# The first two dense halves take the input times the norm's weights, and the norm's factor is applied at their eviction

## The reference, cut to what matters

```python
def rms_norm(x, g):
    y = x * lax.rsqrt(jnp.mean(x * x, axis=-1, keepdims=True) + EPS)
    return y * g

h = rms_norm(x, norm_g[0])
proj = h @ w_in          # its first 1024 columns are lru_x, the next 1024 lru_g, then the rest
xc = causal_conv(lru_x, conv_w) + conv_b      # per channel, 4 taps
...                      # gates, scan, two other mixers, ffn, two more layers
```

## Time and profile before

| | us |
|---|---|
| median of 3 runs | 2349.78 (2349.71 to 2351.39) |
| the profiled execution | 2353.49 |
| its span in the trace | 2351.7 |
| PE busy | 2281.4 (97%) |
| DVE busy | 1474.1 (63%) |
| ACT busy | 919.0 (39%) |

### The profile page before, as it was taken

How to read it: one execution, slowest core, us unless ns; L and a number is a source line. 1 busy time by engine, 2 the same in 40 slices (tenths; PEclk the granted TensorE clock), 3 DMA queues, 4 the chain that set the end, 5 groups by cost and what they waited for, 6 DMA issues and landing times.

```text
span 2351.7 us, 33475 instructions
## 1 busy us (share of the span) xinstructions
PE 2281.4 (97%) x14276; PEld 1983.6 (84%) x14276; DVE 1474.1 (63%) x1936; ACT 919.0 (39%) x1331; POOL 248.5 (11%) x238
## 2 busy tenths in 40 slices
PE   8899998999999999999999999999999999998999
PEld 7899885789998888888859888888888888978998
DVE  6585548577768776756877776335754433976554
ACT  6653435454454222124454212223322222545443
POOL 0030000201111101010020101000100101201110
PEclk9999998899999999999999999999999999999999
DMA  6544370356654454433202544223454322622543
GB/s 239 188 178 163 128 261 33 125 198 233 238 192 167 161 210 187 171 126 113 108 1 108 215 170 188 108 76 114 187 197 162 143 99 84 177 72 93 195 180 108
DMA packets 35393, 358.24 MB, mean 152 GB/s; under 512 B 4029, under 2 KB 6269, under 8 KB 9004
## 3 DMA queue, kind: packets, MB, share of 16 engines
q1 hardware_dynamic: 31788, 343.54, 38.9%
q0 software_dynamic: 3456, 12.56, 1.9%
HBM read 353.11 MB, written 1.13 MB: 151 GB/s over the span
## 4 chain that ended last, share of the span: by engine, by line
PE 88%; DVE 7%; ACT 3%; issue 1%; DMA 1%; POOLq 0%; SPq 0%; DVEq 0%; ACTq 0%
PE psum L861 25%; PE psum L860 25%; PE psum L862 25%; PE psum L924 2%; PE psum L923 2%; PE psum L925 2%; PE psum L1200 1%; PE psum L1226 1%; DVE ring_r L1938 1%; PE psum L1271 1%; DVE rr L1948 1%; DVE small L2465 1%; DVE zT L1967 1%; PE psum L1155 1%; DVE zT_r L1978 0%
## 5 line engine op out<-in xcount | busy, mean ns | idle before, releaser
L860 PE MATMUL psum<-arena_r 128*128 128x256 f32 (+1 forms) x3144 | 1058.8, 337 | 10.4 <-DVE ring_r L1938 4.3
L862 PE MATMUL psum<-arena_r,ring_r 128*128 128x256 f32 (+1 forms) x3144 | 1052.7, 335 | 0.0
L861 PE MATMUL psum<-zT_r,arena_r 128*128 128x256 f32 (+1 forms) x2592 | 848.4, 327 | 0.0
L1440 ACT ACTIVATE arena_r<-ring 128x2048 fp32r<-128x2048 f32 (+1 forms) x252 | 473.3, 1880 | 700.3 <-PE psum L862 651.2
L1938 DVE TENSOR_TENSOR ring_r<-ring,arena_r 128x2048 fp32r<-128x2048 f32 (+1 forms) x252 | 569.5, 2261 | 215.4 <-ACT arena_r L1440 214.5
L860 PEld LDWEIGHTS psum<-arena_r 128*128 128x128 f32 x3144 | 592.2, 188 | 85.7 <-issue 13.1
L862 PEld LDWEIGHTS psum<-arena_r,ring_r 128*128 128x128 f32 x3144 | 595.1, 189 | 65.3
L861 PEld LDWEIGHTS psum<-zT_r,arena_r 128*128 128x128 f32 x2592 | 489.6, 189 | 43.9
L861 PE MATMUL psum<-arena_r 128*128 128x256 f32 (+1 forms) x1128 | 373.4, 331 | 0.0
L2091 DVE CUSTOM_DVE_ANT_0 psum<-arena,cb 128x1024 f32<-128x1024 f32 x256 | 318.0, 1301 | 0.0
L861 PEld LDWEIGHTS psum<-arena_r 128*128 128x128 f32 x1128 | 212.4, 188 | 22.1
(11 more groups left out here) (316 smaller groups left out, 2234.3 us busy)
## 6 DMA issues: line engine op xcount, KB each, us to landing
ring<-in_wf SPq DMA_DIRECT2D x75, 2048.0 KB, 7.6
ring<-in_w SPq DMA_DIRECT2D x41, 2048.0 KB, 7.7
arena<-in_w SPq DMA_DIRECT2D x72, 1024.0 KB, 9.5
ring<-in_wf SPq DMA_DIRECT2D x10, 1536.0 KB, 6.5
ring<-in_w SPq DMA_DIRECT2D x5, 1024.0 KB, 5.3
arena<-strip_scratch POOLq DMA_DIRECT2D x1, 2048.0 KB, 9.5
arena<-rpb_scratch POOLq DMA_DIRECT2D x16, 128.0 KB, 11.3
xT<-in_x SPq DMA_DIRECT2D x1, 1024.0 KB, 5.7
```

The lines of the kernel that those rows point to most:

```text
L860: mm(b[c][:, at], whc, xh[:, k, at], start=(k == ks[0]), stop=False)
L861: mm(b[c][:, at], whc, xl[:, k, at], start=False, stop=False)
L862: last = mm(b[c][:, at], wlc, xh[:, k, at], start=False, stop=(k == ks[-1]))
L1440: A(W_hi[h % NHI][:, 0:n], ring[:, half_slot(h)], ACT.Identity).then_inc(sig("w_hi"), 1)
```

## The change

The norm's tile `norm0` and its eight matmuls go. Instead:

- The DMA queue of SP has the first half of chunk 0 right behind the one-hot table, then the 8 columns of weights of the first norm by themselves (`first_gain_in`), then `x`, the constants, the rest of `vec`, and the second half of chunk 0 as before.
- ACT begins with `w_hi(0)`, makes 8 high parts of `x * g` (`F_hi`), the 8 squares, `w_hi(1)`, loads the table of the root, takes the root (`first_root`), makes `w_hi(2)`, and only then the 8 `z_high`.
- DVE makes `w_lo(0)`, 8 low parts of `x * g` (`F_lo`), adds the squares up itself (7 adds), makes `w_lo(1)`, the reciprocal, evicts the two tiles of `lru_x0` times the factor (`first_x(0)`), makes `w_lo(2)`, goes through the ten rounds of `norm_z` and `z_low`, and evicts `lru_x1` in the same way.
- PE does halves 0 and 1 on `F_hi` and `F_lo`, with one product of ones and the summed squares before the seventh tile of features; halves 2 to 7 and all others on the normed input as before.

```diff
     add("strip", None, "V")
-    add("norm0", None, "A")
-    split_pairs("lru_x", 2, W8_LRU_X, "AA")
+    split_pairs("lru_x", 1, W8_LRU_X, "VV")
+    split("lru_x2", "lru_x3", w8(W8_LRU_X + 1), "AA")
...
+        F_hi, F_lo = part(18456, KT, S), part(20504, KT, S)
+        first_total = psum[:, 7 * BANK:7 * BANK + S]
...
-        PE_SUM = (0, 2, 4)
-        SUMS = (5, 6, 7, 8, 9), (4, 5, 6, 7, 8)
+        PE_SUM = (2, 4)
+        SUMS = (0, 5, 6, 7, 8, 9), (4, 5, 6, 7, 8)
...
-            sp.dma_start(cst[:, 0:CST_FIRST], d["cst"][:, 0:CST_FIRST]).then_inc(sig("cst_in"), 16)
-            sp.dma_start(xT[:, :, 0:S], d["x"].rearrange("k p t -> p k t")).then_inc(sig("x_in"), 16)
             arr, idx, _ = CHUNKS[0][0]
             sp.dma_start(ring[:, 0:HALF], d[arr][idx, :, 0:HALF]).then_inc(sig("first_half_in"), 16)
-            sp.dma_start(vec[:, :], d["vec"]).then_inc(sig("vec_in"), 16)
+            sp.dma_start(V("norm_g", 0, KT), d["vec"][:, 0:KT]).then_inc(sig("first_gain_in"), 16)
+            sp.dma_start(xT[:, :, 0:S], d["x"].rearrange("k p t -> p k t")).then_inc(sig("x_in"), 16)
+            sp.dma_start(cst[:, 0:CST_FIRST], d["cst"][:, 0:CST_FIRST]).then_inc(sig("cst_in"), 16)
+            sp.dma_start(vec[:, KT:VN], d["vec"][:, KT:VN]).then_inc(sig("vec_in"), 16)
...
-            norm(0)
+            def first_ready(k):
+                pe.wait_ge(sig("first_lo"), k + 1)
+                if k == 6:
+                    pe.wait_ge(sig("cst_in"), 16)
+                    pe.wait_ge(sig("norm_sum_x"), 1)
+                    mm(first_total, C("ones"), rr[:, 0:S], start=True, stop=True).then_inc(sig("first_total"), 1)
+
+            split_features(HALF_AT["lru_x0"], S, F_hi, F_lo, before=first_ready, both=True)
+            split_features(HALF_AT["lru_x1"], S, F_hi, F_lo)
             pe.wait_ge(sig("vec_in"), 16)
-            for c in range(4):
...
+            for c in range(2, 4):
+                split_features(HALF_AT[f"lru_x{c}"], S, h_hi, z_lo, before=split_ready(0, 0) if c == 2 else None,
+                               both=c == 2)
...
+            w_hi(0)
+            act.wait_ge(sig("first_gain_in"), 16)
+            act.wait_ge(sig("x_in"), 16)
+            for k in range(KT):
+                A(F_hi[:, k, :], xT[:, k, 0:S], ACT.Identity, scale=V("norm_g", k, 1)).then_inc(sig("first_hi"), 1)
+            for k in range(KT):
+                square(0, k, HALF_TOK[0], xT, "norm_sq")
+            w_hi(1)
             act.wait_ge(sig("cst_in"), 16)
             sqrt_table()
-            norm(0, xT, lambda k: act.wait_ge(sig("x_in"), 16), before=lambda: w_hi(0))
-            w_hi(1)
+            act.wait_ge(sig("first_total"), 1)
+            A(rt[:, 0:S], first_total, ACT.Sqrt, scale=1.0 / D, bias=C("eps")).then_inc(sig("first_root"), 1)
+            w_hi(2)
+            z_high(0, 0)
             act.wait_ge(sig("vec_in"), 16)
...
             def lru_x(c):
-                copy_tiles(f"lru_x{c}", 2, lambda j: A_xp[:, 2 * c + j, 3:S + 3])
+                if c >= 2:
+                    copy_tiles(f"lru_x{c}", 2, lambda j: A_xp[:, 2 * c + j, 3:S + 3])
...
+            w_lo(0)
+            dve.wait_ge(sig("first_gain_in"), 16)
             dve.wait_ge(sig("x_in"), 16)
-            w_lo(0)
-            norm(0, xT, lambda k: V("norm_g", k, 1))
+            for k in range(KT):
+                dve.wait_ge(sig("first_hi"), k + 1)
+                v.scalar_tensor_tensor(out=F_lo[:, k, :], in0=xT[:, k, 0:S], scalar=V("norm_g", k, 1),
+                                       in1=F_hi[:, k, :].bitcast(f32), op0=ALU.mult, op1=ALU.subtract)\
+                    .then_inc(sig("first_lo"), 1)
+            for k in range(1, KT):
+                add_square(0, k, HALF_TOK[0])
             w_lo(1)
+            dve.wait_ge(sig("first_root"), 1)
+            recip(HALF_TOK[0])
...
+            first_x(0)
+            w_lo(2)
+            for k in range(KT + 2):
...
+            norm_over()
+            first_x(1)
+            dve.wait_ge(sig("vec_in"), 16)
```

More of the change, by code:

```diff
@@ L985, in _ @@
             mm(b[0:16, 0:384], K_tbl[0:33, :], oh[0:33, :], start=True, stop=True).then_inc(filled, 1)
-            pe.wait_ge(sig("cst_in"), 16)
-            norm(0)
+            def first_ready(k):
[6 more added lines that the diff above has]
+            split_features(HALF_AT["lru_x1"], S, F_hi, F_lo)
             pe.wait_ge(sig("vec_in"), 16)
-            for c in range(4):
-                split_features(HALF_AT[f"lru_x{c}"], S, h_hi, z_lo, before=split_ready(0, 0) if c == 0 else None,
-                               both=c == 0)
+            for c in range(2, 4):
+                split_features(HALF_AT[f"lru_x{c}"], S, h_hi, z_lo, before=split_ready(0, 0) if c == 2 else None,
+                               both=c == 2)
             for c in range(4):
@@ L1442, in square @@
             def square(q, k, at, src, sem):
-                if k == 0 and q not in PE_SUM:
+                if k == 0 and q > 0 and q not in PE_SUM:
                     act.wait_ge(sig("norm_recip"), q)
@@ L2224, in _, with first_x @@
             v.tensor_copy(K_strip[0:16, :], b[0:16, 0:384]).then_inc(evac["V"], 1)
-            dve.wait_ge(sig("vec_in"), 16)
-            dve.wait_ge(sig("cst_in"), 16)
             link(v.memset(A_xp[:, :, 0:3], 0.0))
             v.memset(mod_[:, :], 0.0)
+            w_lo(0)
+            dve.wait_ge(sig("first_gain_in"), 16)
             dve.wait_ge(sig("x_in"), 16)
-            w_lo(0)
-            norm(0, xT, lambda k: V("norm_g", k, 1))
-            w_lo(1)
+            for k in range(KT):
[5 more added lines that the diff above has]
+                add_square(0, k, HALF_TOK[0])
+            w_lo(1)
+            dve.wait_ge(sig("first_root"), 1)
+            recip(HALF_TOK[0])
+            def first_x(c):
+                for j in range(2):
+                    b = empty(TILE[f"lru_x{c}"] + j)
+                    v.tensor_tensor(out=A_xp[:, 2 * c + j, 3:S + 3], in0=b[:, 0:S], in1=rr[:, 0:S], op=ALU.mult)\
+                        .then_inc(evac["V"], 1)
+            first_x(0)
+            w_lo(2)
+            for k in range(KT + 2):
+                if k < KT:
+                    v.scalar_tensor_tensor(out=zT[:, k, 0:S], in0=xT[:, k, 0:S], scalar=V("norm_g", k, 1),
+                                           in1=rr[:, 0:S], op0=ALU.mult, op1=ALU.mult).then_inc(sig("norm_z"), 1)
+                if k >= 2:
+                    z_low(0, k - 2, 0)
+            norm_over()
+            first_x(1)
+            dve.wait_ge(sig("vec_in"), 16)
             def lo(stage):
```

## The result

| | us |
|---|---|
| kernel before, median of 18 runs | 2349.76 (2347.5 to 2356.52) |
| changed kernel, median of 18 runs | 2355.05 (2350.8 to 2358.92) |
| ratio, with its 95% interval | 1.0015 (1.0008 to 1.0022) |
| profiled execution before, and its span | 2353.49, 2351.7 |
| profiled execution after, and its span | 2353.59, 2351.8 |

The change does not make the kernel faster. It is slower by 3.5 us (1.9 to 5.2) by the ratio, 5.3 us by the medians. Forecast were +2.6 us and 2352.4, in a range up to 2356.5. The two profiled executions are equally long and say nothing of the total (the last experiment shows why); their starts can be read against each other.

The account below looks back on a forecast made before the run. PE alone was taken to bound 18.64 to 67.38, so the end of half 7 decides. Half 3 starting 0.6 us late plus 2.0 for the slow clock gives 2349.78 + 2.6 = 2352.4, range 2348.0 to 2356.5.

Parts of the forecast that it names:

- Half 0: At the start: `x` lands at 9.9, `F_hi` takes 3.3 us, PE starts half 0 at 11.8 instead of 18.64.
- The second rival: DMA of `x` at the start lands up to 2.1 us later, at 12.0; time 2354.5 or about 2355.6; chance 0.15.
- Half 1: Second half of chunk 0 lands at 15.6, `w_hi(1)` from 15.8, PE on half 1 from about 20.4 until 26.2.
- The third rival: ACT's new switch to the root's table costs 1.28 us beyond its load, 1.0 on the path: 2353.4; chance 0.04.
- Half 2: DVE's rounds begin at 24.9 instead of 16.86; PE runs half 2 from 26.7 to 32.5, a gain of 5.7 us.
- Half 3: On ACT `w_hi(3)` stands behind `z_high`, `lam` and taps; PE pauses 6.3 us, half 3 starts at 38.8, 0.6 late.
- The first rival: Half 3 follows half 2 at once, at 32.5 and full clock; half 7 ends 5.7 us earlier, time 2344.1; chance 0.09.
- The clock: Behind PE's pause half 3 begins at 1.2 GHz; 2.4 or 1.2 us lost, 2.0 taken.
- a side remark: On PE, the granted clock falls within 3.2 us of the last matmul, read from two falls in the profile before.
- The sum: End of half 3 comes 0.6 + 2.0 = 2.6 us later, so the time is 2349.78 + 2.6 = 2352.4.
- the term for the start of half 3: PE starts half 3 at 38.8 against 38.2 before: 0.6 us late.
- Costed at nothing: Behind half 3: DVE's later convolutions (at most 0.5 us), `w_lo(4)` ready during slow half 3, and POOL's later DMA of `x_tok`.

Follow-up runs that it names:

- the last experiment: The kernel before and the changed kernel each ran twice more, unchanged; whole executions 2353.49, 2349.53, 2351.29 before and 2353.59, 2353.62, 2356.29 after.
- the kernel with filled pause: Changed kernel plus 40 matmuls that nobody needs on PE before half 3; measured 2352.0, ratio to the kernel before 1.0004.
- the kernel with the padding tile: Changed kernel plus a tiny tile in the place of `norm0`, so later tiles keep their PSUM banks of before; measured 2355.72, ratio 1.0021.

## Why the prediction was right, and where not

**Half 0.** Predicted from 11.8, measured 11.69. `x` landed at 9.3 (9.9 predicted), and `F_hi` took 3.30 as the row of the same size said. The second rival, `x` late, is refuted: it needed 12.0. What it feared from the small pieces did not come; the megabyte of `x` took 7.2 us from issue to landing behind a megabyte of weights.

**Half 1.** I put the second half of chunk 0 at 15.6 since it has the same bytes ahead; it landed at 13.5, a miss of 2.1 us. It cost the sum little, as `w_hi(1)` then waited for the squares and ran from 15.03 (15.8 predicted). The first weights landed at 6.2 (7.0 predicted).

**The table.** The load at 16.95 took 1.28 and the next operation ran at 18.24; the root ended at 18.81, before DVE was through with `w_lo(1)` at 19.6. The third rival is refuted. The Trainium skill, "ScalarE: Activation LUTs", section "What ACT_TABLE_LOAD costs", adds about 1380 ns of drain to a switch. This trace does not show it: 0.02 us stood between the copy before and the load, 0.01 us between the load and the next operation.

**Half 2.** Predicted from 26.7 to 32.5, measured 25.93 to 31.89. The rounds began 0.7 us earlier than I had them: `w_lo(1)` ended at 19.6 instead of 20.0, and the two evictions took 0.76 instead of 0.84.

**Half 3.** The step that carries the forecast held: the chain `z_high`, `lam` (29.46 to 32.69, 3.23 us), taps, `w_hi(3)`, `w_lo(3)` put half 3 at 38.8 and the pause at 6.3; measured 38.11 and 6.22. The first rival, half 3 at once behind half 2, is refuted as a description of this kernel, and it is nearly what the kernel with `w_hi(3)` early does (a pause of 1.25, 2346.81 against the 2344.1 of the rival). It was right to ask what stands in ACT's list rather than how busy ACT is (39%).

**The clock.** Forecast 2.0 us lost. The slow time of half 3 was 4.6, 5.9 and 4.0 us in the three executions, which at 0.44 is 2.0, 2.6 and 1.8; the kernel with filled pause gives 1.9. The longest of them still shows half the clock here, where the first came back (second execution of the changed kernel):

```profile
42.00:44.00 2.00, 2.00 (x11) 2.00 (x11) 1.94 (x3) 0.38 (x1) 0.00 (x0) 0.50 0.00 0
```

What failed is a side remark: I said that the clock falls within 3.2 us of the last matmul. In the five executions with a pause of 6.2 us it fell 2.5 to 5.3 us after it (the stretches that hold the fall, weighed by their clock). Nor does the length of the pause alone decide. With the work on `lam` late, a pause of 3.01 us left the clock up. In the kernel before, a pause of the same length ends at 511.43, and from 512.2 the clock was at half for 10 us. PE's row, and a stretch behind it:

```profile
511.43 2.87 PE L887 MATMUL psum<-cst,arena 128*128 128x128 f32 x14 [3.01 <-DVE arena L2196]
```

```profile
514.00:522.00 8.00, 5.95 (x25) 4.89 (x24) 6.37 (x18) 5.18 (x13) 0.00 (x0) 0.50 0.46 193
```

**The sum.** I had half 3 of before at 38.2, an estimate from ACT's row. PE's matmuls of before put it at 38.39, right behind the last matmul of half 2, whose tile ACT picks up at 38.59:

```profile
38.27 0.28 PE L862 MATMUL psum<-xT_r,ring_r 128*128 128x256 f32 x1
38.39 0.28 PE L860 MATMUL psum<-xT_r,arena_r 128*128 128x256 f32 x1
```

So the term for the start of half 3 was +0.6 and measured -0.3 (38.11), and the clock's term was right with 2.0: half 3's last tile is 1.75 us later (46.10 to 44.35). At the chain DMA 1.3 us are left of it in the first pair, and 1.65 over three. The missing 0.4 us is PE's pace, at full clock in both: the four halves from there to the chain DMA took 23.04 us before and 22.61 in the changed kernel. This too scatters within one kernel (22.75 in the second execution of each), so it is no gain of the change. The sum of the terms was 0.95 to 1.3 us too high at the place where it was made. The total is nevertheless above it (+3.5 by the ratio, interval 1.9 to 5.2, which holds the 2.6). The step that nothing here shows is that the total moves by what the start moves: it moved by 1 to 3.6 us more, and that remains open. That the forecast lies so near the measured time is partly luck, two misses of opposite sign. The base was a single profiled execution 3.7 us above the median; only differences within its first 70 us were taken from it, which repeat within 1.3 us. Two figures beside the sum were added up wrongly: with the root at 21.1 the sum would have been 3.7, not 3.8, and the second rival at its worst 2355.8, not 2355.6.

**Costed at nothing.** The convolutions and `w_lo(4)` behind the slow half 3, and POOL's later load of `x_tok`: in the changed kernel PE has no new gap between half 3 and the chain DMA, so these held.

## What to carry to other kernels

A lead on the busiest engine lasts only as far as its helpers' lists carry it: follow each list up to the first operation that was not moved, here one copy of 1.9 us behind eight small operations and two table loads, and move that too. Having it ahead turned the change from 0.15% slower to 0.2% faster, and a pause that can't be avoided should be kept short, since the clock can charge again for it (at the start it did for pauses of 4.19 and 6.22 us, not for one of 3.01). When two single profiles are compared, compare the stretch that the change touches; here the totals of two executions of the same kernel differed by 4 us.

## What I had not expected of the hardware

**POOL stops DVE.** In the kernel with `w_lo(3)` on POOL, the first of DVE's operations L2282 took 4750 ns where the others of its kind took 470. It has two inputs in SBUF, as has POOL's subtraction, and it ended about when POOL's did (28.72). `w_lo(2)`, which DVE had begun 1.3 us before POOL began, took its usual 2.28 us. Count, and minimum, median and maximum in ns, of the five up to 30.8:

```profile
L2282 DVE SCALAR_TENSOR_TENSOR zT<-xT,vec,rr x5: 470/472/4750, 24.3 to 30.8; 128x256 f32<-128x256 f32 x5
```

So POOL's idle time was no free time: DVE saved the 2.28 us of `w_lo(3)` and paid 4.28 in waiting. The Trainium skill, "SBUF — State Buffer", section "SBUF: two separate sides", says that such a pair of operations shares one pair of ports as an exclusive lock, which the one that starts first holds for its whole instruction. This trace agrees: 4.75 us for 0.47 behind POOL, and no slowdown of `w_lo(2)`, which was first.

**The clock's return scatters.** Behind one and the same pause of 6.22 us, the slow time was between 3.1 us (in the kernel with the padding tile) and 5.9 us. Between 303 and 463 us such differences made up to 3.4 us in one kernel, as much as the whole change was worth.
